# Final multiplies of three tiles on ScalarE and gpsimd, and gathered rows counted in two halves

## What is computed

```python
def rms_norm(x, g):
    xf = x.astype(jnp.float32)
    y = xf * lax.rsqrt(jnp.mean(xf * xf, axis=-1, keepdims=True) + RMS_EPS)
    return (y * g.astype(jnp.float32)).astype(x.dtype)
...
    h = h + moe_ffn(rms_norm(h, ffn_norm_g), w_rg, b_rg, w_re, b_re, w_eg, w_eu, w_ed)
...
    y_prompt = rms_norm(hp, final_norm_g)
    y_sample = rms_norm(hs, final_norm_g)
```

## Time and profile before

| | us |
|---|---|
| median of 3 runs | 1063.06 (1063.02 to 1064.12) |
| the profiled execution, its own time | 1064.89 |
| its span in the trace | 1063.3 |
| TensorE busy | 959.8 (90%) |
| VectorE busy | 373.5 (35%) |
| ScalarE busy | 184.8 (17%) |
| gpsimd busy | 212.5 (20%) |

### The profile page before, as it was taken

The page is one execution under the profiler, slowest core; times in us unless marked ns, Lnnn a source line. Parts: engine busy times, 40 slices in busy tenths (PEclk is TensorE's granted clock), DMA queues, the critical chain, the costliest instruction groups (busy, mean ns, idle before and its releaser), DMA issues.

```text
span 1063.3 us, 13611 instructions
## 1 busy us (share of the span) xinstructions
PE 959.8 (90%) x5391; PEld 600.7 (56%) x5391; DVE 373.5 (35%) x845; ACT 184.8 (17%) x418; POOL 212.5 (20%) x307
## 2 busy tenths in 40 slices
PE   6989999999999999999998899999878878877985
PEld 6744444777776656774553465665545545544651
DVE  3169999976541112330155120111011011011117
ACT  3143110323343335001120000000000000000003
POOL 2740651242211110000001121111101111111121
PEclk9999999999999999999998999999999999999898
DMA  9920212221207553923038999999999999999996
GB/s 344 394 106 1 79 36 91 86 90 69 80 1 238 214 183 104 364 103 157 39 135 330 421 420 424 421 420 425 423 421 426 423 423 422 426 422 424 420 413 220
DMA packets 53821, 282.81 MB, mean 266 GB/s; under 512 B 8815, under 2 KB 9683, under 8 KB 33159
## 3 DMA queue, kind: packets, MB, share of 16 engines
q1 hardware_dynamic: 43095, 245.72, 57.6%
q0 software_dynamic: 10624, 36.44, 9.4%
q10 hardware_dynamic: 56, 0.01, 0.0%
HBM read 266.89 MB, written 22.65 MB: 272 GB/s over the span
## 4 chain that ended last, share of the span: by engine, by line
PE 55%; DMA 27%; ACT 2%; issue 1%; DVE 1%; SPq 1%; POOL 0%; POOLq 0%; ACTq 0%; DVEq 0%
DMA arena<-in_w_exp_up 25%; PE psum L838 6%; PE psum L1011 6%; PE psum L860 5%; PE psum L675 5%; PE psum L1029 5%; PE psum L1122 5%; PE psum L1123 5%; PE psum L1140 3%; PE psum L1114 2%; PE psum L982 1%; PE psum L948 1%; PE psum L906 1%; PE psum L932 1%; PE psum L1053 1%
## 5 line engine op out<-in xcount | busy, mean ns | idle before, releaser
L1122 PE MATMUL psum<-arena 128*64 128x256 f32 x960 | 165.0, 401 | 33.9 <-DMA arena<-in_w_exp_up 33.9
L1123 PE MATMUL psum<-arena 128*64 128x256 f32 x960 | 162.8, 395 | 0.0
L1140 PE MATMUL psum<-arena 128*64 128x512 f32 x512 | 116.9, 597 | 17.7 <-ACT arena L1451 17.7
L1122 PEld LDWEIGHTS psum<-arena 128*64 128x64 f32 x960 | 80.1, 142 | 82.6 <-DMA arena<-in_w_exp_up 43.5
L1870 DVE TENSOR_TENSOR arena<-arena,psum 128x256 f32<-128x256 f32 x32 | 13.5, 421 | 265.0 <-ACT arena L1447 265.0
L1123 PEld LDWEIGHTS psum<-arena 128*64 128x64 f32 x960 | 94.9, 144 | 16.1 <-issue 1.8
L675 PE MATMUL psum<-arena 128*128 128x512 f32 x192 | 84.5, 594 | 0.2 <-ACT arena L1323 0.2
L1447 ACT ACTIVATE arena<-psum 128x256 f32<-128x256 f32 x32 | 12.3, 383 | 407.8 <-PE psum L1123 374.3
L1140 PEld LDWEIGHTS psum<-arena 128*64 128x64 f32 x512 | 40.4, 136 | 72.1 <-issue 72.1
L2149 POOL CAST arena<-arena 128x1 int32 x30 | 5.5, 183 | 314.2 <-DVE arena L1880 314.2
L838 PE MATMUL psum<-arena 128*128 128x288 f32 x256 | 66.6, 411 | 0.0
(11 more groups left out here) (326 smaller groups left out, 1170.4 us busy)
## 6 DMA issues: line engine op xcount, KB each, us to landing
arena<-in_w_exp_down SPq DMA_DIRECT2D x32, 2048.0 KB, 35.5
arena<-in_w_exp_gate SPq DMA_DIRECT2D x28, 2048.0 KB, 31.7
arena<-in_w_exp_up SPq DMA_DIRECT2D x19, 2048.0 KB, 36.4
arena<-in_w_exp_up SPq DMA_DIRECT2D x26, 1024.0 KB, 31.1
arena<-in_w_in SPq DMA_DIRECT2D x7, 2048.0 KB, 8.3
y_d<-arena SPq DMA_DIRECT2D x1, 8192.0 KB
arena<-in_w_exp_gate SPq DMA_DIRECT2D x7, 1024.0 KB, 12.0
arena<-in_x_prompt SPq DMA_DIRECT2D x8, 512.0 KB, 6.8
```

Source lines behind the costliest of these rows:

```text
L1122: pe.matmul(bank(2 + s, 256, rows), x_k, gate, start=(k == 0), stop=(k == KD - 1), skip_group_check=True)
L1123: last = pe.matmul(bank(2 + s, 256, rows, 256), x_k, up, start=False, stop=(k == KD - 1), skip_group_check=True)
L1140: last = pe.matmul(bank(4 + s, 512, slice(at_row, at_row + 64)), hT[s][:, k % 2, CAP * (k // 2):CAP * (k // 2) + CAP], wd[j][:, k, 512 * h ...
```

## The change

Five things are changed at the end of the kernel.

- *Two semaphores for a tile's gathers.* The upper rows stay on `s_y[i]`. The lower rows count on `s_lo[i]`, which is one of the page semaphores, and `add_both` waits for `PAGES[i] + 16` there before its first add and for 16 on `s_y[i]` before its second.
- *Tiles 0, 1 and 2 are finished without VectorE's multiply.* ScalarE copies the sum from PSUM to `yg[n][0]`, scaled by the reciprocal root, and gpsimd multiplies that by `fgrow` into `yout[n]`. ScalarE's copy of tile 0 stands behind the root of tile 1, those of tiles 1 and 2 behind the root of tile 2.
- *VectorE's order.* The reciprocals (`root`) of tiles 0, 1 and 2 stand behind the adds of tiles 1, 2 and 3. Then come the adds of tile 4, and reciprocal and multiply of tiles 3 and 4.
- *A further wait.* The second add of tile 4 waits for the copy of tile 0, whose banks it overwrites.
- *Shared counts.* gpsimd's multiplies count on the old `rope_done` and ScalarE's copies on the old `gs_done`, both renamed; all earlier waits on them keep their numbers.

```diff
+        POOL_FIN = 3
+        GATE_SIG = 2 * KD
...
-        s_idx = sem("idxpage_in")
-        s_kin = [sem(f"kpage_in{b}") for b in range(2)]
-        s_vin = [sem(f"vpage_in{b}") for b in range(2)]
+        s_idx = sem("idxpage_lo4_in")
+        s_kin = [sem(f"kpage_lo{b}_in") for b in range(2)]
+        s_vin = [sem(f"vpage_lo{2 + b}_in") for b in range(2)]
+        s_lo = s_kin + s_vin + [s_idx]
+        PAGES = [16 * (DB // 2)] * 4 + [16 * DB]
...
             for i in range(TILES):
-                sp.wait_ge(S["fin_ready"], i + 1)
+                if i < POOL_FIN:
+                    sp.wait_ge(S["rope_fin_done"], len(JOBS) + i + 1)
+                else:
+                    sp.wait_ge(S["fin_ready"], i - POOL_FIN + 1)
                 sp.dma_start(y_rows[i], yout[i][0:rows_of(i), :]).then_inc(S["y_out"], 16)
...
                 act.activation(rt3[0:r, i:i + 1], ss3[0:r, i:i + 1], ACT.Sqrt, bias=eps[0:r], scale=1.0 / D).then_inc(S["rt3"], 1)
+                for n in {1: (0,), 2: (1, 2)}.get(i, ()):
+                    act.wait_ge(S["rs3"], n + 1)
+                    act.activation(yg[n][0], psum[:, SUM_BANK[n] * 512:SUM_BANK[n] * 512 + D], ACT.Copy, scale=rstd3[:, n:n + 1]).then_inc(S["gs_fs_done"], 1)
...
-            def final(i):
-                r = rows_of(i)
-                if i == 0:
-                    dve.wait_ge(S["late_in"], 96)
+            def root(i):
+                r = rows_of(i)
                 dve.wait_ge(S["rt3"], i + 1)
                 dve.reciprocal(rstd3[0:r, i:i + 1], rt3[0:r, i:i + 1]).then_inc(S["rs3"], 1)
+
+            def final(i):
+                r = rows_of(i)
+                dve.wait_ge(S["late_in"], 96)
                 dve.wait_ge(S["rs3"], i + 1)
                 dve.scalar_tensor_tensor(yout[i][0:r, :], psum[0:r, SUM_BANK[i] * 512:SUM_BANK[i] * 512 + D], rstd3[0:r, i:i + 1], fgrow[0:r, :], ALU.mult, ALU.mult).then_inc(S["fin_ready"], 1)
 
             def add_both(i):
-                dve.wait_ge(s_y[i], 32)
+                dve.wait_ge(s_lo[i], PAGES[i] + 16)
                 add_rows(i, 0, wi_lo).then_inc(S["y_comb"], 1)
+                dve.wait_ge(s_y[i], 16)
                 dve.wait_ge(S["y_comb"], 2 * i + 1)
...
+                if i == 4:
+                    dve.wait_ge(S["gs_fs_done"], GATE_SIG + 1)
...
-            for i in range(3):
+            add_both(0)
+            for i in range(1, TILES):
                 add_both(i)
-            final(0)
-            for i in range(3, TILES):
-                add_both(i)
-            for i in range(1, TILES):
+                if i <= POOL_FIN:
+                    root(i - 1)
+            for i in range(POOL_FIN, TILES):
+                root(i)
                 final(i)
...
-                                            bounds_check=EARLY - 1, oob_is_err=False).then_inc(s_y[i], 16)
+                                            bounds_check=EARLY - 1, oob_is_err=False).then_inc((s_lo, s_y)[k][i], 16)
...
+            pool.wait_ge(S["late_in"], 96)
+            for i in range(POOL_FIN):
+                pool.wait_ge(S["gs_fs_done"], GATE_SIG + i + 1)
+                pool.tensor_tensor(yout[i], yg[i][0], fgrow, ALU.mult).then_inc(S["rope_fin_done"], 1)
```

More of the change, by code:

```diff
@@ L391, in program @@
         s_x = [sem(f"x_in{i}") for i in range(TILES)]
-        s_y = [sem(f"y_rows_in{i}") for i in range(TILES)]
+        s_y = [sem(f"y_hi_rows_in{i}") for i in range(TILES)]
         s_res = sem("resid_in")
@@ L514, in _ @@
             load_ring(8)
-            sp.wait_ge(S["gs_done"], 1 + len(gb_raw))
+            sp.wait_ge(S["gs_fs_done"], 1 + len(gb_raw))
             for i in range(TILES):
@@ L721, in turn @@
             def turn(job, n_blocks, rows, width):
-                pe.wait_ge(S["rope_done"], job + 1)
+                pe.wait_ge(S["rope_fin_done"], job + 1)
                 b = t_bank()
@@ L1257, in take_qi @@
                 if job >= 2:
-                    act.wait_ge(S["rope_done"], job - 1)
+                    act.wait_ge(S["rope_fin_done"], job - 1)
                 b = QI_BANK[i]
@@ L1422, in _ @@
             act.wait_ge(S["son_done"], DB // 2)
[L1423 removed]
+            act.activation(sgA[0], sgA[0], ACT.Sigmoid).then_inc(S["gs_fs_done"], 1)
             for k in range(KD):
[L1425 removed]
+                act.activation(sgB[k], gb_raw[k], ACT.Sigmoid).then_inc(S["gs_fs_done"], 1)
             for k in range(1, KD):
[L1427 removed]
+                act.activation(sgA[k], sgA[k], ACT.Sigmoid).then_inc(S["gs_fs_done"], 1)
             for i in range(TILES):
@@ L1625, in take_fast @@
                 if g == 0:
-                    dve.wait_ge(S["rope_done"], len(JOBS))
+                    dve.wait_ge(S["rope_fin_done"], len(JOBS))
                     for s in range(2):
@@ L1934, in _ @@
                 for i in range(TILES):
-                    dve.wait_ge(s_y[i], 48)
+                    dve.wait_ge(s_y[i], 32)
             with dve.Else():
                 dve.nop()
+            def root(i):
+                r = rows_of(i)
+                dve.wait_ge(S["rt3"], i + 1)
+                dve.reciprocal(rstd3[0:r, i:i + 1], rt3[0:r, i:i + 1]).then_inc(S["rs3"], 1)
             def final(i):
                 r = rows_of(i)
-                if i == 0:
-                    dve.wait_ge(S["late_in"], 96)
-                dve.wait_ge(S["rt3"], i + 1)
-                dve.reciprocal(rstd3[0:r, i:i + 1], rt3[0:r, i:i + 1]).then_inc(S["rs3"], 1)
+                dve.wait_ge(S["late_in"], 96)
                 dve.wait_ge(S["rs3"], i + 1)
@@ L2038, in _ @@
                 if job:
-                    pool.wait_ge(S["rope_done"], job)
+                    pool.wait_ge(S["rope_fin_done"], job)
                 if job >= 2:
@@ L2061, in _ @@
                     last = pool.tensor_tensor(heads_of(out, r, n), heads_of(rtmp[0], r, n), heads_of(rtmp[1], r, n), ALU.add)
-                last.then_inc(S["rope_done"], 1)
+                last.then_inc(S["rope_fin_done"], 1)
                 if kind == "qi":
@@ L2171, in combine @@
                     if k:
-                        pool.wait_ge(s_y[i], 32)
+                        pool.wait_ge(s_y[i], 16)
                     gather(yg[i][k][0:r, :], rows, dest[0:r, k, i:i + 1], done[i])
```

8 lines of the change are left out of this document (4 added, 4 removed).

## The result

| | before | changed |
|---|---|---|
| median, same chip | 1063.15 (1061.43 to 1064.76, 11 runs) | 1066.17 (1065.33 to 1070.23, 11 runs) |
| profiled execution, own time | 1064.89 | 1068.82 |
| its span | 1063.3 | 1067.2 |

The ratio is 1.0038 with an interval of 1.0028 to 1.0048: slower, by 3.0 us in the medians and 3.9 between the profiled executions. Up to ScalarE's copy of the last expert's rows the two spans agree within 0.11 us (that copy starts at 1039.51 and now at 1039.62), so the rest of the 3.9 is in the tail.

What follows compares the result with a forecast made beforehand. It took the tail's chain of waits, from tile 3's gathered rows through VectorE, TensorE and ScalarE, as the bound. The middle of +6.6 and +3.7, +5.2 us, on the 1063.06 median gave 1068.3; range 1065.2 to 1070.4.

Steps and rivals of the forecast that it cites:

- two branches: Tile 2's matmuls: +6.6 us without a lower clock there; at 1.2 GHz +3.0 or +4.4, middle 3.7.
- exclusion: VectorE's adds with two SBUF inputs and gpsimd's multiplies wait for each other's whole instruction; +3.0 to +6.6 us, chance 0.84.
- tile 3's second add and tile 4's adds with 2.5 to 3.7 us: Sign expected in VectorE's timeline after the change: these adds stretched beside gpsimd's multiplies, instead of 1.3 us.
- tile 4's matmuls at 58 to 60: Sign expected on TensorE: these matmuls start at 58 to 60, where they stood at 55.00.
- Rival A: VectorE's adds are not held by gpsimd's multiplies; -0.8 to +0.6 us, 1062.3 to 1063.7, chance 0.09.
- rival B: VectorE is always served before gpsimd's multiplies; +0.5 or +1.9 us, 1063.6 to 1065.0, chance 0.04.
- The order of turns: Tiles 3 and 4: multiplies and adds alternate, holding both tile 4 adds; its matmuls at 1060.15, or 1058.0 with slow tile 2.
- A multiply: On gpsimd, 128x1024 with both inputs in SBUF: 2.36 us, bounds 1.27 and 2.62; the first asks at 48.10.
- The lower rows: Tile 3's lower gathered rows are in by 47.9, so its first add starts earlier; gain up to one add, 1.32 us.
- Reciprocal 0: On VectorE, waits for ScalarE's root ahead of tile 2's adds: first add at 45.20, matmuls at 47.87 (before 47.05).
- ScalarE's copies: Three copies of 1024 columns from PSUM, 1.05 us each; bounds for one are 0.58 and 1.2.
- TensorE's clock: Over 5 us of idle puts tile 4's matmuls at 1.2 GHz, 1.41 us more; for tile 2 left open.

Runs made afterwards that it cites:

- e3: Changed kernel with gpsimd's three multiplies replaced by memsets of the same size, which read no SBUF; median 1063.78, ratio 1.0013.
- e2: Changed kernel with gpsimd's three multiplies held back until all ten of VectorE's adds are done; median 1068.91, ratio 1.0066.
- e5: Changed kernel with the adds turned, so that the second add reads PSUM and has one SBUF input; median 1066.58, ratio 1.0030.
- e9: Changed kernel with a tile's first add waiting for the upper rows too; median 1067.38, ratio 1.0047.
- e6: Changed kernel with reciprocal 0 behind tile 2's adds and reciprocals 1 and 2 behind tile 3's; median 1067.31, ratio 1.0050.
- e4: Kernel before with one 128x1 memset at the end of gpsimd's queue, waiting for tile 4's root; median 1068.40, ratio 1.0052.
- e7: Changed kernel with only tile 0 finished by ScalarE and gpsimd, tiles 1 and 2 by VectorE again; median 1063.26, ratio 1.0011.
- e1: Kernel before with only the lower rows' own semaphores and their waits added; median 1061.73, ratio 0.9991.
- e8: Kernel before with the lower rows' own semaphores, plus two filler matmuls on TensorE before tile 3's; median 1061.16, ratio 0.9992.
- e10: Kernel before with one 128x1 memset on gpsimd right behind its last gather, without a wait; 1065.94, one run.

## Why the prediction was right, and where its steps were not

The class was right (slower, 0.85), and 1066.17 is inside the range of 1065.2 to 1070.4; but 1068.3 was 2.1 us too high, and the sum was wrong in two places of opposite sign: the chain through VectorE lost 2.3 us, not 5.2, and a term that I had at nothing cost 1.6 more. These are the 3.9 us between the profiled executions; the 3.0 of the medians are the better size, since the profiled one of the changed kernel stood 2.7 above its median and that of before 1.7. So the number owes something to luck. The forecast was also the middle of two branches, and the one that came about (tile 2 kept 2.4 GHz) was the one with +6.6 us, for which the chain was 4.3 too long. And "slower" alone does not speak for exclusion: by the estimate under e3 the DRAIN alone would have made the kernel some 2.3 us slower. Exclusion is shown by the lengths of the adds in the runs, not by the time.

Of the signs that were named, "tile 3's second add and tile 4's adds with 2.5 to 3.7 us" held for one of the three (1.29, 1.26 and 2.85), and tile 4's matmuls at 58 to 60 did not come (1056.25). The held add of tile 3 was its first, and the adds of 1.3 us in the changed kernel are those that did not ask during a multiply: tile 3's second, asked 1.2 us after the end of multiply 0, and tile 4's first, 0.06 us ahead of multiply 1.

- **Exclusion itself** held, with the reading from which it was taken: e2, e3 and e5 separate the cases by gpsimd's reads and VectorE's inputs. The Trainium skill (SBUF — State Buffer, section "Who interferes with whom") states it by the inputs: a VectorE instruction with two of them in SBUF contends with a GpSimd instruction that reads SBUF, not with one that only writes it. The traces agree, now also for an add that writes PSUM (2.42 and 2.85 us) and for the memsets (1.26 to 1.29). Rival A, no exclusion for such adds, is refuted by these rows, and rival B, VectorE always first, by tile 4's second add, held 1.57 us.
- **The order of turns** is the step that failed: "Copy 1 ended at 52.42, multiply 1 asked at 52.50: it runs 52.83 to 55.19, the add 55.19 to 56.47". VectorE's first add of tile 4 asked at 1051.99 and multiply 1 at 1052.05, so the add went first and only one of tile 4's two was held. Its matmuls began at 1056.25, where I had 1060.15 or 1058.0. The two asked 0.06 us apart; with the order the other way about both are held, which was 1.7 us in e9. My sum, too, had them 0.4 us apart (52.93 and 52.50), which is less than it was wrong by, and should have carried both orders.
- **A multiply** took 1.99 us, not the 2.36 of the earlier trace rows, and multiply 0 asked at 1047.56, not 48.10, because TensorE was sooner through tiles 0 and 1 (tile 1's square at 1044.96, not 45.55). So it came ahead of tile 3's first add and held that (by 1.05 us) instead of the second, another order that came out the other way; that tile's matmuls began at 1052.07, where I had 1052.88. The Trainium skill's 2.6 cycles an element (GPSIMD Engine Reference, section 3.1), an estimate of 2.2 us, lies between; the measurement decides.
- **The lower rows** were in 0.4 us later than "in by 47.9", and the add was then held by multiply 0 anyway.
- **Reciprocal 0** moved tile 2's first add to 1044.80 (forecast 45.20) and its matmuls to 1047.51 (47.87): right. e6 takes it away, and the time stays.
- **ScalarE's copies**: 1.10 and 2.35 for two, against 1.05 each.
- **TensorE's clock**: tiles 2 and 3 kept 2.4 GHz after 2.58 us of idle each, where 2.64 us had been followed by 1.2 GHz; tile 4, after 2.20 us, fell within its matmuls, and took about 1.0 us more, where I had 1.41 or nothing. The length of the idle before was not enough to forecast from.
- **"Alone they would be free: the stores of tiles 0 to 2 are not last"** was false. A store order was looked at, but not what an engine owes at the program's end. By e4 a single late instruction of gpsimd costs 5.7 us in the median; with G at 27.4 and S at 25.8, it is 1.6 us of this change on top of VectorE's chain. It is in fact the end by itself: the 2.3 us of that chain are hidden behind it, and count only as far as held turns also delay gpsimd's last multiply. e5 shows this, with VectorE 1.8 us earlier and the end 0.7. It would stay with no exclusion at all, as the estimate under e3 says, so Rival A's time of -0.8 to +0.6 was too low as well. No run has all three multiplies meeting no add at their old places, so how the 3.0 us divide between the two causes stays an estimate.

## What to carry to other kernels

Before giving an idle engine the last bit of work, read the closing line of the trace: how long that engine's DRAIN takes and what it has in front of it. In this kernel gpsimd's last compute instruction has to end 9 us ahead of the program's end, and its last gather has to land 4.5 us ahead. Between gpsimd's instructions that read SBUF and VectorE's with two SBUF inputs, count each meeting as one whole instruction of the other engine, write down who asks first, and where the two are closer than the error of the sum, carry both orders.

## What the runs showed of the hardware

- gpsimd's final DRAIN ended 8.92 us after its last compute instruction in the changed kernel, in e2 to e7 and in e9, be it a multiply of 1.99 us or a memset of 0.10; in the kernel before, e1, e8 and e10 it ended 4.5 us after the landing of the last gather. The DRAINs of TensorE, ScalarE and VectorE outlasted their work by about 0.05 us. What gpsimd does in that time was not found out.
- gpsimd multiplies 128x1024 in 1.99 us, 1.94 ns a column, where additions of other forms gave 2.12 between two widths.
- The same idle of 2.57 to 2.58 us before tile 2's matmuls was followed by 1.98 us for them in the changed kernel (granted clock 1.00), by 2.51 in e7 (mean 0.77), 2.58 in e3 (0.75) and 3.13 in e5 (0.61). An idle stretch's length alone did not tell the price of the clock; with tile 3's idle filled (e8), its matmuls and tile 4's ran at 1.00.
